# Hybrid attention/convolution encoder layer: the front's sums and low parts all on VectorE, the first block's parts in halves, the second half's rows loaded a step ahead, the convolution behind the third sum

## The chip, the core and the metric

One NeuronCore of a Trainium2 chip runs the whole program in one launch. Its engines are PE (TensorE, matmul), DVE (VectorE), ACT (ScalarE), POOL (GpSimd) and SP (SyncE, which here only issues DMAs). Each runs its own instruction stream in order, and they meet only at semaphores. The metric is the device time of one execution in microseconds, the median of three runs. The profile is a separate execution.

## The reference, cut to what matters

The input is (1, 2048, 1024) in float32. The part of the reference that the change touches is the first norm and the combined projection:

```python
u = rms_norm(x, norm_mix_g[l])
proj = jnp.einsum('bsd,de->bse', u, w_in[l])
q, k, v, bg, cg, hv = jnp.split(proj, ...)          # six parts, each 512 wide
conv = bg * short_conv(cg * hv, conv_w[l])          # centred, width 3, over positions
```

Behind it, outside the change: differential attention over 4 heads with a T5 bias, an RMS norm per head, the output projection with a residual sum, a SwiGLU feed-forward of width 2816 with a residual sum, and a last RMS norm.

## The kernel before, in words

**Precision.** Every float32 matrix product is done as three fp32r products: an operand is split into a high part (ACT copies it to fp32r) and a low part (DVE subtracts the high part from the original), and PE adds hi*hi + hi*lo + lo*hi. So PE needs the low part of an operand, and a low part needs its high part from ACT first.

**The front.** The projection is done for the two halves of the sequence (1024 positions each, of two blocks b = 0, 1 of 512). The 1024 channels are two halves kh = 0, 1 of 4 k-tiles of 128. For the first half, the normed input u is made in place in four tiles `u_raw[b][kh]` of 128 x 2048: `scale_x` (DVE, four instructions of 128 x 512) multiplies by the gain and by 1/rms, which PE has spread over the partitions (`spread_r`). Four output tiles (q) are made plainly: `plain_product(b, tile)`, 24 matmuls each, whose u operands are the splits of the four blocks (`split_block`). `keep_plain` takes each result out of PSUM.

All other output tiles are made in pairs with 7 block products in place of 8: `pair_product(s, k)` for k = 0..6, 12 matmuls each, where s = 0..21 is a step over one pair and one half. Its u operands are three of the blocks and four sums t1..t4 of blocks (`u_slot[k]` holds high and low part of operand k; k = 3, 1, 2, 5 are t1..t4). Before, POOL makes the four sums of the first half (lines 780 to 785), 128 x 2048 each, and `split_sum` splits them (ACT high, DVE low).

**Inside a step** DVE works through a fixed list, `front_step(s)`: the low parts of the seven weight operands of the next step (`split_pair(s + 1, k)`), the sums of the next weights (`sum_pair`), and the sums of the results, `make_u_2`, `make_u_3`, `make_c_22`, `make_c_21`, `make_c_12`, which PE waits for: product k = 5 waits for u_3, k = 6 for c_22, and the next step's k = 2 and 3 for c_21 and c_12. A step whose pair is an input of the convolution is "gated"; `convolve(s)` runs in the step behind it (s = 3, 4, 6, 7 and 17, 18, 20, 21), before directly behind `make_u_2`. In an "out" step (s = 4, 7, 18, 21) `gate_out` multiplies the convolution's result by the third projection, and the next step's first product waits for its first call.

**The second half's input** is made while steps 0 to 8 run. SP loads a row tile (`load_row(n)`, one buffer), ACT squares it (`square`), DVE and POOL make the inverse root (`mean`, `inverse_root`), PE spreads it (`spread_r` in odd steps, behind k = 2). POOL's `make_blocks(i)`, i = 0..3, loads a piece of x (1 MB), issues the DMAs of the scaled blocks to DRAM, makes four sums of 128 x 512 (lines 803 to 809) once DVE has scaled the piece (`scale_piece(i)`, in step 2i + 1), stores the sums, and waits for these stores before it loads the next piece. `load_row(s)` and `load_row(s + 1)` both stand in the even steps of SP's list.

**The turn.** In step 9 SP loads the seven operands of the second half from DRAM (`load_next(k)`, 1 MB each); ACT makes the high parts, DVE the low parts of k = 0, 2, 4, 6 and POOL those of k = 1, 3, 5 (line 820). Step 10 is the first to use them.

The orders are all written out by hand. Behind the front stand attention (PE, DVE, ACT and POOL), the output projection and the feed-forward; the change doesn't touch their code.

## Time and profile before

| | |
|---|---|
| median of 3 runs | 2680.53 us (2679.77 to 2682.09) |
| profiled execution, its own time | 2678.98 us |
| span of that execution | 2677.2 us |
| busy: PE, DVE, ACT, POOL | 97%, 65%, 42%, 22% |
| mean granted TensorE clock | 0.992 |

The span is the time from the first to the last instruction; what lies around it is 1.8 us. The front ends when PE starts on attention, 522 us into the span. A matmul's record shows more than its share of PE's time, because matmuls overlap; the time from one start to the next is what one costs. "Idle before" on a row is how long the engine stood, and what stands behind the arrow is what ended it.

### The profile page before, as it was taken

To read this page: it belongs to the slowest core of one execution; us is meant where nothing else is said; L and a number is where in the kernel's file an instruction comes from. 1 tells how busy PE (TensorE), PEld (TensorE's weight loads), DVE (VectorE), ACT (ScalarE), POOL (GpSimd) and SP (SyncE) were. 2 spreads that over 40 slices of the span, in tenths; PEclk is the share of its full clock that TensorE was granted. 3 is DMA by queue.
4 is the path that set the end of the run, shared out by engine and by line. 5 is a ranking of instruction groups with operands and counts; after the bars stand their busy time and mean duration, and the time that the engine had idled before them with its cause. 6 is when DMAs were issued, how large, how long until landed. Compare 5 with 4: busy or idle time off the path is not lost. (4 is left out here: it accounts for less than half of the span.)

```text
span 2677.2 us, 34138 instructions
## 1 busy us (share of the span) xinstructions
PE 2585.3 (97%) x11920; PEld 2115.3 (79%) x11920; DVE 1739.7 (65%) x2559; ACT 1122.1 (42%) x1588; POOL 586.2 (22%) x394
## 2 busy tenths in 40 slices
PE   7899899989999999999999999999999999999998
PEld 5778788767777777788888888878888888888887
DVE  6788867678888788744476666676566643434354
ACT  4433432266777677632343333343333322323232
POOL 4123200077777777700000000000000000000000
PEclk9999999999999999999999999999999999999999
DMA  6645641412131211156763222342222235656564
GB/s 242 185 170 177 219 149 67 111 45 62 44 82 48 59 44 48 64 169 210 234 189 118 74 90 74 122 150 92 75 90 74 90 134 143 196 158 206 146 209 125
DMA packets 239122, 333.66 MB, mean 125 GB/s; under 512 B 15888, under 2 KB 151568, under 8 KB 234032
## 3 DMA queue, kind: packets, MB, share of 16 engines
q1 hardware_dynamic: 233664, 313.45, 38.4%
q0 software_dynamic: 4544, 17.83, 1.8%
q8 instruction: 56, 0.92, 0.1%
q10 hardware_dynamic: 816, 1.12, 0.1%
q14 instruction: 42, 0.34, 0.0%
HBM read 240.07 MB, written 92.27 MB: 124 GB/s over the span
## 5 line engine op out<-in xcount | busy, mean ns | idle before, releaser
L2136 PE MATMUL banks<-z_hi,w_hi 128*128 128x512 f32 x1116 | 434.5, 389 | 2.3 <-DVE u L1710 1.8
L2136 PE MATMUL banks<-z_hi,w_lo 128*128 128x512 f32 x1116 | 434.2, 389 | 0.0
L2136 PE MATMUL banks<-z_lo,w_hi 128*128 128x512 f32 x1116 | 434.1, 389 | 0.0
L836 POOL TENSOR_TENSOR exp<-exp,exp 128x2048 f32<-128x2048 f32 x64 | 295.8, 4621 | 5.3
L865 POOL TENSOR_TENSOR y_rstd<-y_mean,neg_half 128x1 f32<-128x1 f32 x16 | 9.7, 605 | 1305.8 <-DVE y_mean L1865 1305.8
L1056 ACT ACTIVATE exp<-exp,neg_max 128x2048 f32<-128x2048 f32 x128 | 257.2, 2010 | 34.6 <-DVE neg_max L1583 33.4
L1968 PE MATMUL projected<-u_hi,pair_w_hi 128*128 128x512 f32 x616 | 243.5, 395 | 21.1 <-DVE u_f L1375 7.4
L1160 ACT ACTIVATE w_hi<-w_sum 128x512 fp32r<-128x512 f32 x176 | 111.0, 632 | 328.5 <-PE banks L2136 320.9
L2136 PEld LDWEIGHTS banks<-z_hi,w_hi 128*128 128x128 f32 x1116 | 209.5, 188 | 47.3 <-issue 2.8
L2136 PEld LDWEIGHTS banks<-z_lo,w_hi 128*128 128x128 f32 x1116 | 209.5, 188 | 43.5
L2136 PEld LDWEIGHTS banks<-z_hi,w_lo 128*128 128x128 f32 x1116 | 209.5, 188 | 43.3
L1968 PE MATMUL projected<-u_lo,pair_w_hi 128*128 128x512 f32 x616 | 242.2, 393 | 0.0
L1968 PE MATMUL projected<-u_hi,pair_w_lo 128*128 128x512 f32 x616 | 241.9, 393 | 0.0
L1850 DVE TENSOR_TENSOR hid_lo<-hid_raw,hid_hi 128x512 fp32r<-128x512 f32 x88 | 60.9, 693 | 243.7 <-ACT hid_hi L1258 243.7
L2193 PE MATMUL banks<-down_hi,hid_hi 128*128 128x512 f32 x704 | 216.8, 389 | 0.6 <-DVE down_lo L1853 0.6
L2193 PE MATMUL banks<-down_lo,hid_hi 128*128 128x512 f32 x704 | 216.8, 389 | 0.0
L2193 PE MATMUL banks<-down_hi,hid_lo 128*128 128x512 f32 x704 | 216.7, 389 | 0.0
L1066 ACT ACTIVATE a_t_hi<-tile_turned 128x512 fp32r<-128x512 f32 x256 | 148.1, 600 | 158.8 <-PE tile_turned L2022 158.7
L1595 DVE TENSOR_TENSOR a_t_lo<-tile_turned,a_t_hi 128x512 fp32r<-128x512 f32 x256 | 172.0, 687 | 53.7 <-ACT a_t_hi L1066 53.6
L2004 PE MATMUL scores<-k_sum,q_part_hi 128*128 128x512 f32 x512 | 178.0, 429 | 15.1 <-DVE neg_max L1583 8.4
L1258 ACT ACTIVATE hid_hi<-hid_raw 128x512 fp32r<-128x512 f32 x88 | 55.6, 631 | 320.1 <-PE banks L2193 320.1
L1583 DVE CUSTOM_DVE_ANT_0 exp<-scores,window,half_min 128x1024 f32<-128x1024 f32 x128 | 163.8, 1280 | 31.4 <-PE scores L2004 25.8
(204 smaller groups left out, 5001.3 us busy)
## 6 DMA issues: line engine op xcount, KB each, us to landing
down_raw<-in_w_down SPq DMA_DIRECT2D x88, 512.0 KB, 4.4
pair_raw<-in_w_in SPq DMA_DIRECT2D x24, 1024.0 KB, 6.1
gate_raw<-in_w_gate SPq DMA_DIRECT2D x44, 512.0 KB, 4.5
up_raw<-in_w_up SPq DMA_DIRECT2D x44, 512.0 KB, 5.5
hidden_t<-hid_stage SPq DMA_DIRECT2D x88, 256.0 KB, 2.6
hid_raw<-hidden_t SPq DMA_DIRECT2D x88, 256.0 KB, 3.7
projected_t<-hi_out SPq DMA_DIRECT2D x36, 256.0 KB, 2.8
row_tile<-in_x SPq DMA_DIRECT2D x16, 512.0 KB, 6.1
```

The lines of the kernel that those rows point to most:

```text
L836: nc.gpsimd.tensor_tensor(exp_0[:, slot_0], exp_0[:, slot_0], exp_1[:, slot_1], ALU.add).then_inc(mixed_ready, 1)
L1056: nc.scalar.activation(rows, rows, ACT.Exp, scale=-1.0, bias=neg_max[:, t % 2, part:part + 1], accum_out=exp_sum[:, part, t % 16:t % 16 + ...
L1066: nc.scalar.activation(dst, turned_bank(h, t, index), ACT.Copy).then_inc(group_hi, 1)
L1160: nc.scalar.activation(w_slot[k][0][:, :, :], src, ACT.Copy).then_inc(w_hi_ready_2, 1)
L1258: nc.scalar.activation(hid_part[slot][0][:, :], hid_raw[:, slot], ACT.Copy).then_inc(f_hi_ready, 1)
L1583: nc.vector.tensor_tensor_reduce(out=rows[:, half * HALF:(half + 1) * HALF], in0=scores[:, unit % 2], in1=window[:, window_slice(t, half)] ...
L1595: nc.vector.tensor_tensor(parts[1][at], turned_bank(h, t, index), parts[0][at].bitcast(FP32), ALU.subtract).then_inc(group_lo, 1)
L1850: nc.vector.tensor_tensor(hid_part[slot][1][:, :], hid_raw[:, slot], hid_part[slot][0][:, :].bitcast(FP32), ALU.subtract).then_inc(f_lo_re ...
L1968: last = nc.tensor.matmul(projected[:, PRODUCT_BANK[k]], pair_w[k][w][:, kt], u_slot[k][u][:, kt], start=(kt == 0 and n == 0 and k < 4), s ...
L2004: last = nc.tensor.matmul(scores[:, unit % 2, b * BANK:(b + 1) * BANK], q_part[n][:, (t // 4) % 2, part, t % 4 * P:(t % 4 + 1) * P], k_sum ...
L2136: last = nc.tensor.matmul(c_bank[BANK_OF[k]], w_slot[k][w][:, kt], block[z][:, kt], start=(kt == 0 and t == 0 and k < 4), stop=(kt == 3 an ...
L2193: last = nc.tensor.matmul(y_banks[j][:, c * BANK:(c + 1) * BANK], hid_part[slot][h][:, j * P:(j + 1) * P], down_part[slot][w][:, c * BANK: ...
```

## The change

- `sum_u(n)`: the four sums of the first half move from POOL to DVE, in the order t1, t2, t3, t4 (before: t1, t2, t4, t3), behind the splits of the second block's operands. `u_raw` is placed in other slots, so that each sum can be split while the others are still needed.
- `split_half_block(n)`: `scale_x` of the first block signals after each half (two k-tiles), and its splits go in halves of 128 x 1024 on ACT and DVE. PE waits for them half by half.
- `sum_piece(i)`: the four sums of a piece move from POOL to DVE, to step 2i + 2, where DVE first waits for the stores of the blocks.
- `load_row` of rows 2, 4, 6 moves to the step before (s = 1, 3, 5), ahead of the last stores of that step.
- `split_next(1)`, `(3)`, `(5)` move from POOL to DVE.
- `convolve(s)` moves from behind `make_u_2` to behind `make_c_22`.

```diff
-            b11, b21, b12, b22 = (u_raw[b][kh][:, :, :] for b in range(2) for kh in range(2))
-            nc.gpsimd.tensor_tensor(t1, b12, b11, ALU.subtract).then_inc(u_summed, 1)
...
-                pool.wait_ge(block_stored, 48 * (i + 1))
-                nc.gpsimd.tensor_tensor(p11, p12, p11, ALU.subtract).then_inc(u_summed, 1)
...
+                pool.wait_ge(u_summed, 4 + 4 * i + 4)
...
+            def sum_piece(i):
+                dve.wait_ge(block_stored, 48 * (i + 1))
+                p11, p21, p12, p22 = (piece[:, b, 4 * kh:4 * kh + 4] for b in range(2) for kh in range(2))
+                done = 4 + 4 * i
+                nc.vector.tensor_tensor(p11, p12, p11, ALU.subtract).then_inc(u_summed, 1)
+                dve.wait_ge(u_summed, done + 1)
+                nc.vector.tensor_tensor(p12, p22, p12, ALU.subtract).then_inc(u_summed, 1)
...
@@ SP, front_step(s)
-                if s < 8 and s % 2 == 0:
-                    load_row(s)
+                if s == 0:
+                    load_row(0)
...
                     store_pieces(s, 2, 3)
+                if s < 7 and s % 2:
+                    load_row(s + 1)
@@ DVE, front_step(s)
                 make_u_2(s)
-                convolve(s)
                 if later:
                     split_pair(s + 1, 1)
                 if s == TURN:
-                    split_next(6)
+                    split_next(5)
                 make_u_3(s)
                 if later:
                     split_pair(s + 1, 2)
                 make_c_22(s)
+                if s == TURN:
+                    split_next(6)
+                convolve(s)
+                if s < 9 and s and s % 2 == 0:
+                    sum_piece(s // 2 - 1)
@@ PE, plain_product and pair_product
-                    if tile == 0 and kt % 4 == 0:
-                        pe.wait_ge(u_lo_ready, 2 * b + kt // 4 + 1)
+                    if tile == 0 and kt % 4 == 0 and b:
+                        pe.wait_ge(u_lo_ready, 4 + kt // 4 + 1)
+                    if tile == 0 and kt % 2 == 0 and not b:
+                        pe.wait_ge(u_lo_ready, kt // 2 + 1)
...
-                    if k % 2:
-                        pe.wait_ge(u_lo_pool, k // 2 + 1)
-                    else:
-                        pe.wait_ge(u_lo_ready, 8 + k // 2 + 1)
+                    pe.wait_ge(u_lo_ready, 10 + k + 1)
```

DVE's list at the start of the program before: the two halves of the channels of the first block are scaled (`u_raw_63`, `u_raw_64`), then split into `u_lo_50` and `u_lo_58`.

```order
L1305 SCALAR_TENSOR_TENSOR u_raw_63<-u_raw_63,gain,r_wide 128x512 x4
L1292 SCALAR_TENSOR_TENSOR plain_w_lo_82<-pair_raw_106,plain_w_hi_81 128x1024
L1305 SCALAR_TENSOR_TENSOR u_raw_64<-u_raw_64,gain,r_wide 128x512 x4
L1322 TENSOR_TENSOR u_lo_50<-u_raw_63,u_hi_49 128x2048
L1322 TENSOR_TENSOR u_lo_58<-u_raw_64,u_hi_57 128x2048
```

The same place now:

```order
L1285 SCALAR_TENSOR_TENSOR u_raw_63<-u_raw_63,gain,r_wide 128x512 x4
L1272 SCALAR_TENSOR_TENSOR plain_w_lo_82<-pair_raw_106,plain_w_hi_81 128x1024
L1333 TENSOR_TENSOR u_lo_50<-u_raw_63,u_hi_49 128x1024 x2
L1285 SCALAR_TENSOR_TENSOR u_raw_64<-u_raw_64,gain,r_wide 128x512 x4
L1333 TENSOR_TENSOR u_lo_58<-u_raw_64,u_hi_57 128x1024 x2
```

The first low parts now stand ahead of the second scaling, as two instructions of half the width.

DVE's list in step 4 (and 7), from the sum u_2 (`u_f<-projected,u_f`, first row) on, before:

```order
L1370 TENSOR_TENSOR u_f<-projected,u_f 128x512
L1436 COPY edges<-gated 128x2
L1438 TENSOR_SCALAR conv_y<-gated,taps 128x1023
L1441 SCALAR_TENSOR_TENSOR conv_y<-gated,taps,conv_y 128x1022
L1444 SCALAR_TENSOR_TENSOR conv_y<-gated,taps,conv_y 128x1023
L1364 SCALAR_TENSOR_TENSOR pair_w_lo_92<-pair_sum,pair_w_hi_91 128x512
L1375 TENSOR_TENSOR u_f<-projected,u_f 128x512
L1364 SCALAR_TENSOR_TENSOR pair_w_lo_94<-pair_sum,pair_w_hi_93 128x512
L1381 TENSOR_TENSOR lo_out<-projected,u_f 128x512
```

In step 4 now, from the split behind u_2 on (L1392 is u_3, L1398 is c_22, L1473 the first `gate_out`):

```order
L1381 SCALAR_TENSOR_TENSOR pair_w_lo_92<-pair_sum,pair_w_hi_91 128x512
L1392 TENSOR_TENSOR u_f<-projected,u_f 128x512
L1381 SCALAR_TENSOR_TENSOR pair_w_lo_94<-pair_sum,pair_w_hi_93 128x512
L1398 TENSOR_TENSOR lo_out<-projected,u_f 128x512
L1453 COPY edges<-gated 128x2
L1455 TENSOR_SCALAR conv_y<-gated,taps 128x1023
...
L1311 TENSOR_TENSOR piece<-piece 128x512
L1313 TENSOR_TENSOR piece<-piece 128x512
L1315 TENSOR_TENSOR piece<-piece 128x512
L1317 TENSOR_TENSOR piece<-piece 128x512
L1381 SCALAR_TENSOR_TENSOR pair_w_lo_96<-pair_sum,pair_w_hi_95 128x512
L1381 SCALAR_TENSOR_TENSOR pair_w_lo_98<-pair_raw_107,pair_w_hi_97 128x512
L1473 TENSOR_TENSOR conv_y<-projected,conv_y 128x512
```

The convolution and the four piece sums now stand together between c_22 and the first `gate_out`.

DVE's list at the turn, from the end of step 9 into step 10, before (`u_lo_4_58` is the low part of operand 4, `u_3_f_105` is u_3):

```order
L1396 TENSOR_TENSOR lo_out_115<-projected,u_2_f_104 128x512
L1364 SCALAR_TENSOR_TENSOR pair_w_lo_6_102<-pair_sum_108,pair_w_hi_6_101 128x512
L1352 TENSOR_TENSOR pair_sum_108<-pair_raw_1_107 128x512
L1354 TENSOR_TENSOR pair_sum_108<-pair_sum_108,pair_raw_1_107 128x512
L1334 TENSOR_TENSOR u_lo_4_58<-u_lo_4_58,u_hi_4_57 128x2048
...
L1370 TENSOR_TENSOR u_2_f_104<-projected,u_2_f_104 128x512
L1364 SCALAR_TENSOR_TENSOR pair_w_lo_1_92<-pair_sum_108,pair_w_hi_1_91 128x512
L1334 TENSOR_TENSOR u_lo_6_62<-u_lo_6_62,u_hi_6_61 128x2048
L1375 TENSOR_TENSOR u_3_f_105<-projected,u_2_f_104 128x512
```

The same place now:

```order
L1351 TENSOR_TENSOR u_lo_3_56<-u_lo_3_56,u_hi_3_55 128x2048
L1413 TENSOR_TENSOR lo_out_115<-projected,u_2_f_104 128x512
L1381 SCALAR_TENSOR_TENSOR pair_w_lo_6_102<-pair_sum_108,pair_w_hi_6_101 128x512
L1369 TENSOR_TENSOR pair_sum_108<-pair_raw_1_107 128x512
L1371 TENSOR_TENSOR pair_sum_108<-pair_sum_108,pair_raw_1_107 128x512
L1351 TENSOR_TENSOR u_lo_4_58<-u_lo_4_58,u_hi_4_57 128x2048
...
L1387 TENSOR_TENSOR u_2_f_104<-projected,u_2_f_104 128x512
L1381 SCALAR_TENSOR_TENSOR pair_w_lo_1_92<-pair_sum_108,pair_w_hi_1_91 128x512
L1351 TENSOR_TENSOR u_lo_5_60<-u_lo_5_60,u_hi_5_59 128x2048
L1392 TENSOR_TENSOR u_3_f_105<-projected,u_2_f_104 128x512
```

Operand 3 is now in DVE's list ahead of the end of step 9, operand 5 has taken the place of operand 6 ahead of u_3, and operand 6 stands behind c_22.

## Rows read from the trace of the kernel before

**Rows 1.** Busy time by window (us busy, instructions), granted clock, DMA share, GB/s.
```profile
13.11:312.15 299.04, 268.04 (x1145) 218.21 (x1146) 252.28 (x321) 114.78 (x167) 95.94 (x67) 0.97 0.57 195
78.50:83.00 4.50, 4.49 (x11) 3.52 (x12) 4.50 (x8) 0.00 (x0) 0.00 (x0) 0.50 0.44 162
```

**Rows 2.** Timeline of PE, waits in the front: start, us, engine, line, operation, [idle before].
```profile
22.06 0.76 PE L1937 MATMUL projected<-u_hi,plain_w_hi 128*128 128x512 f32 x1 [8.96 <-DVE u_lo L1322]
52.26 0.50 PE L1937 MATMUL projected<-u_hi,plain_w_hi 128*128 128x512 f32 x1 [0.97 <-DVE u_lo L1322]
78.52 0.79 PE L1968 MATMUL projected<-u_hi,pair_w_hi 128*128 128x512 f32 x1 [6.92 <-DVE pair_w_lo L1364]
139.30 0.47 PE L1968 MATMUL projected<-u_hi,pair_w_hi 128*128 128x512 f32 x1 [3.48 <-DVE lo_out L1381]
176.79 0.47 PE L1968 MATMUL projected<-u_hi,pair_w_hi 128*128 128x512 f32 x1 [1.39 <-DVE u_f L1375]
216.99 0.47 PE L1968 MATMUL projected<-u_hi,pair_w_hi 128*128 128x512 f32 x1 [1.39 <-DVE u_f L1375]
288.99 0.77 PE L1968 MATMUL projected<-u_hi,pair_w_hi 128*128 128x512 f32 x1 [3.24 <-issue]
304.79 0.63 PE L1968 MATMUL projected<-u_hi,pair_w_hi 128*128 128x512 f32 x1 [4.67 <-DVE u_f L1375]
```

**Rows 3.** Timeline of DVE at the start of the program.
```profile
13.22 2.72 DVE L1305 SCALAR_TENSOR_TENSOR u_raw<-u_raw,gain,r_wide 128x512 f32<-128x512 f32 x4 [3.21 <-PE r_wide L1925]
15.86 1.22 DVE L1292 SCALAR_TENSOR_TENSOR plain_w_lo<-pair_raw,plain_w_hi 128x1024 fp32r<-128x1024 f32 x1
19.63 4.49 DVE L1322 TENSOR_TENSOR u_lo<-u_raw,u_hi 128x2048 fp32r<-128x2048 f32 x2
```

**Rows 4.** Timeline of POOL, the first and the last of its four sums of blocks.
```profile
43.47 6.59 POOL L780 TENSOR_TENSOR u_sum<-u_raw,u_raw 128x2048 f32<-128x2048 f32 x1 [15.89 <-DVE u_raw L1305]
61.65 5.05 POOL L785 TENSOR_TENSOR u_sum<-u_raw,u_raw 128x2048 f32<-128x2048 f32 x1
```

**Rows 5.** Timeline of DVE beside these sums.
```profile
46.46 5.74 DVE L1322 TENSOR_TENSOR u_lo<-u_raw,u_hi 128x2048 fp32r<-128x2048 f32 x1
52.13 0.68 DVE L1340 TENSOR_TENSOR lo_out<-projected,hi_out 128x512 fp32r<-128x512 f32 x1
52.73 4.49 DVE L1352 TENSOR_TENSOR pair_sum<-pair_raw 128x512 f32<-128x512 f32 x1
62.16 5.09 DVE L1356 TENSOR_TENSOR pair_sum<-pair_raw 128x512 f32<-128x512 f32 x1
67.78 2.28 DVE L1329 TENSOR_TENSOR u_lo<-u_sum,u_hi 128x2048 fp32r<-128x2048 f32 x1
```

**Rows 6.** Timeline of ACT, the wait for a row in step 2.
```profile
136.16 1.06 ACT L884 ACTIVATE row_tile<-row_tile 128x1024 f32<-128x1024 f32 x1 [7.04 <-DMA row_tile<-in_x]
```

**Rows 7.** Timeline of DVE, first and behind last instruction of a convolution.
```profile
171.73 0.22 DVE L1436 COPY edges<-gated 128x2 f32<-128x2 f32 x1
175.36 0.69 DVE L1364 SCALAR_TENSOR_TENSOR pair_w_lo<-pair_sum,pair_w_hi 128x512 fp32r<-128x512 f32 x1
```

**Rows 8.** Timeline of POOL, last sum of piece 1, next piece's load, its root.
```profile
167.84 1.62 POOL L809 TENSOR_TENSOR piece<-piece 128x512 f32<-128x512 f32 x1
178.20 0.56 POOL L793 DMA_DIRECT2D piece<-in_x_second  x1 [5.14 <-DMA u_blocks<-piece]
182.03 0.94 POOL L771 TENSOR_TENSOR rstd<-mean_eps,neg_half 128x1 f32<-128x1 f32 x1 [3.27 <-DVE mean_eps L1297]
```

**Rows 9.** Timeline of SP's queue and of ACT at the turn.
```profile
264.03 8.48 SPq L457 DMA_DIRECT2D u_lo<-u_blocks  x4
271.87 1.92 ACT L901 ACTIVATE u_hi<-u_lo 128x2048 fp32r<-128x2048 f32 x1 [1.77 <-DMA u_lo<-u_blocks]
```

**Rows 10.** Timeline of DVE at the turn, the instructions beside POOL's.
```profile
277.33 4.96 DVE L1364 SCALAR_TENSOR_TENSOR pair_w_lo<-pair_raw,pair_w_hi 128x512 fp32r<-128x512 f32 x1
282.81 6.08 DVE L1334 TENSOR_TENSOR u_lo<-u_lo,u_hi 128x2048 fp32r<-128x2048 f32 x1
294.33 5.10 DVE L1364 SCALAR_TENSOR_TENSOR pair_w_lo<-pair_raw,pair_w_hi 128x512 fp32r<-128x512 f32 x1
```

More of the change, by code:

```diff
@@ L1012, in _ @@
             split_plain(0)
-            split_block(0)
-            split_block(1)
+            for n in range(4):
+                split_half_block(n)
             split_plain(1)
@@ L1298, in mean, with scale_x @@
                                         ALU.mult, ALU.add).then_inc(mean_ready, 1)
[L1300 removed]
+            def scale_x(b, kh, kts=range(4)):
                 dve.wait_ge(r_ready, 4 * b + 4)
                 dve.wait_ge(x_loaded[b][kh], 16)
[L1303 removed]
+                for kt in kts:
                     rows = u_raw[b][kh][:, kt]
```

131 lines of the change are left out of this document (73 added, 58 removed).

## Prediction, made before the changed kernel was run

> **What bounds the kernel now.** I began with the windows table, then the timeline of PE alone, reading only the rows that carry an idle time, and then the timelines of DVE, POOL, ACT and SP around each of them. The reader should see that PE is the bound nearly everywhere, so a change can only win where PE stands or runs slowly, and that the front is where it does. From the last instruction that spreads the first root to the end of step 10, PE is busy 268.0 of 299.0 us at a mean granted clock of 0.97 [rows 1]. PE's waits there are eight [rows 2]: 8.96, 0.97, 6.92, 3.48, 1.39, 1.39, 3.24 and 4.67, together 31.0 us. Behind three of them the matmuls also start long (0.79, 0.77, 0.63 us where others start with 0.47): the clock has fallen to its lower level, 1.2 GHz, and the window behind the wait of 6.92 shows it, 0.50, with 11 matmuls in 4.5 us [rows 1]. From 176.79 to 216.99 PE does 14 products of 12 matmuls, one wait of 1.39 and some 0.6 of spreading, so one product is 38.2 / 14 = 2.73 us, a matmul 0.227 and a step of seven products 19.1. At the lower level a matmul costs 0.41.
>
> Why DVE is late in front of the 6.92: POOL's four sums run from 43.47 to 66.7 [rows 4], and DVE's instructions with both inputs in SBUF crawl beside them: a low part of 128 x 2048 takes 5.74 where the same one later takes 2.28, and three of the weight sums (two shown) take 4.5 to 5.1 where 128 x 512 needs 0.6 from start to start [rows 5]. The instruction at 52.13, which has one input in PSUM, takes 0.68 beside the same sum of POOL [rows 5]. The Trainium skill's page "SBUF — State Buffer" (section "Who interferes with whom") has the rule for it: DVE and GpSimd share one pair of ports, as an exclusive lock, which a DVE instruction with two SBUF inputs needs and one with a single one doesn't. By that rule the two engines never worked side by side there at all, so a sum moved to DVE costs its own time and no more; if they had shared bandwidth, moving it would win less. The trace agrees, as far as these rows go.
>
> I set T for the start of a step on PE, and take 0.6 for a DVE instruction of 128 x 512 [rows 5] and 2.24 for one of 128 x 2048 (two in 4.49) [rows 3].
>
> **The change, part by part.**
>
> First block in halves. Before, DVE scales (2.72), does a weight part (1.22), scales again, and has the first low part at about 21.9; PE starts at 22.06 [rows 2, 3]. Now ACT can start on the first half after two of the four scalings (14.6) and is done by 15.7; DVE is through with scaling and weight part at 17.1 [rows 3] and makes a low part of 128 x 1024. No row has that instruction; half of 2.24 is 1.12, the weight part of the same width 1.22 [rows 3]; I take 1.15. PE starts at 18.3, 3.8 us earlier. What is late next: the third quarter, behind one low part, four scalings and one more low part (19.4 + 2.7 + 1.1 = 23.2), while PE, slow at first as now, is through with two quarters at 22.4. It waits 0.8. Gain 3.0.
>
> The sums on DVE. Contention goes: 3.5 us of the low part and 12.9 of the three weight sums, 16.4; four sums of 2.24 come, 9.0. DVE is also 3 us earlier. Counted through: second scaling done at 40.3, two low parts 44.7, `keep_plain` 45.3, four sums to 54.2. The wait of 0.97 goes, since the last low part of the second block is there at 44.7 and PE wants it at 48. `plain_product(1, 3)`, the one that now waits behind the sums (through `keep_plain(0, 3)`, at 54.8), begins at 62. Then to the first three weight parts at 64.3, and PE ends the plain products at 67.3; so step 0 starts at 67.3 against 78.52 and nothing is late: 11.2, of which 3.0 is above and 8.2 here. With the wait of 6.92 gone the clock doesn't fall: 11 matmuls at 0.41 in place of 0.227, 2.2. DVE is through with step 0's parts at about 73, six microseconds after PE has begun, where it was five before; that brings the row for ACT's square, loaded behind them, close to PE's k = 6. I put 0.2 for it, bounds 0 and 2.
>
> Rows a step ahead. In step 2 ACT waits 7.04 for a row [rows 6], which holds up the high part of the third weight operand, c_22 behind it, and PE by 3.48 [rows 2]. Loaded ahead of step 1's last stores the row is some 15 us earlier: 3.5 gained. Nothing stands behind this load in SP's queue but stores with three steps' slack; if the store were late by the 0.4 us of an issue, nobody would ask.
>
> Convolution behind c_22. It is 3.6 us of DVE (171.73 to 175.36) [rows 7], and PE's two waits of 1.39 are for u_3, right behind it [rows 2]. They go: 2.8. In its place the first `gate_out` is late. In step 4, c_22 can't be made before product 3 ends, T + 10.9, so c_22 at T + 11.6, convolution to 15.2, piece sums (four, chained by their semaphores, 0.73 each) to 18.1, two weight parts 19.3, `gate_out` 19.9; the next step wants it at 19.1. Cost 0.8. In step 7, which has 3.2 us of scaling in place of the sums, 1.1 by the same count, because its c_22 is late (below). Steps 18 and 21 have neither sums nor scaling: `gate_out` is there at 17.0.
>
> Piece sums. Before, POOL's last one ends at 169.46, and it issues the next piece's load at 178.20, 8.7 later, with the root behind it [rows 8]. That was early in the step; now the sums end at T + 18.1 in steps 4 and 6. Load issue, two roots (0.56 + 0.94 + 0.55) put the second root at T + 28.9, and PE wants it behind product k = 2 of the next step, T + 19.1 + 8.2 = T + 27.3. The wait: 0.8 in step 5 (it starts 0.8 late anyway) and 1.8 in step 7 (sums a little later). In step 2 there is no convolution, the sums end at 15, and nobody waits. DVE now waits itself for the block stores; behind it stand the weight parts of the next step. The stores have 14 us from the scaling to the sums, and POOL's wait for stores of that kind was 5.1 behind 3.3 of issuing [rows 8], so nothing. The contention in the four pieces (about 4 us of DVE each) goes and pays for the 2.9.
>
> The turn. Before: two waits, 3.24 and 4.67 [rows 2], and 12 and 8 matmuls at the lower clock, 20 x 0.2 = 4.0 plus 0.5 in the change between: 12.4 us. DVE loses 16.1 - 3.4 = 12.7 us beside POOL [rows 10] and now gets three low parts, 6.7. But the seven loads start a little later: the last sums end at T9 - 4.5 (T9: start of step 9), their stores are there at about T9 + 4, where the first load went out at T9 + 2.7 before; 1.3 late. It landed 7.8 after its issue [rows 9]. So ACT's first high part ends at T9 + 13.8 and DVE goes on at 14.4: five low parts, six instructions of 128 x 512 and the next weights' first sums (1.4) bring it to 30.7 for operand 4, and PE wants that at 29.9: wait 0.8. Five short ones with operand 5's low part among them: u_3 at 36.5, PE wants it at 33.5: wait 3.0. Operand 6's low part is there at 39.9: wait 0.7. Together 4.5 in place of 12.4: 7.9. Bounds: 12.4 (no wait is left) and 4 (the clock falls again, and DVE runs 1.5 late).
>
> **The sum.** 3.0 + 8.2 + 2.2 + 3.5 + 2.8 = 19.7; less 0.2 + 0.8 + 1.1 + 0.8 + 1.8 = 4.7; plus 7.9: 22.9. Behind step 10 the steps had no wait of PE, and attention and feed-forward keep their code. The profiled execution took 2678.98, so 2656 in its terms; the median of the runs shown is 1.5 above it: 2657.5.
>
> **A page against the turn's number.** After a wait of 3.24 the clock fell and after one of 3.48 it didn't [rows 2], so the wait of 3.0 that I expect ahead of product 5 may or may not cost it. Taken as a fall, it is 8 to 12 matmuls at 0.41, 1.6 to 2.4 us, and the time 2659.5. The Trainium skill's "TensorE: Matmul & The Clock Gate" (Part 1, "The HAM clock gate") says that an idle PE is throttled to half rate until it has been busy for a while, by a count that runs freely and doesn't start with the wait. By that rule the fall is possible; the trace, with one case of either kind, agrees.
>
> **The rivals.**
>
> A: the pieces' chain is longer. POOL's wait for the stores was 8.7 us in the one shown; with the stores behind row and weight loads it can be 10 or more, and then the piece itself is late for its scaling too, and with it the blocks for step 9. Against it: SP's queue is quieter where the sums now end. Price: 1.4 more in each of steps 3, 5 and 7, 2 in c_21, and 1.4 at the turn: gain 15 to 17, 2664.
>
> B: the turn wins little. The loads share the DMA engines and land later than DVE could use them. For it: ACT waited for the first of them [rows 9]. Against: it didn't for the next three, and DVE was the late one. Then the turn gives 3 in place of 7.9: 2662.
>
> C: nothing takes the place of the waits, because DVE, some 17 us of work lighter than in the contended trace, catches up everywhere: 19.7 + 12.4 less a little: 2650.
>
> D: slower. DVE stands in `sum_piece` for the block stores, in order, with c_21, c_12 and all weight parts behind it. Each microsecond over the 14 that the stores have costs PE nearly one, four times. At 20 us from scaling to landing the whole gain is gone, and from there it is slower; at 24, 2680.5 - 23 + 40 = 2697. Nothing speaks for 20 where such stores took 8.4.
>
> E: the change doesn't do what it says. POOL keeps only roots of 128 x 1 and DMA issues, so it can't contend with sums; that part can't fail. That the half parts win nothing could be, if the second weight half of the block isn't in yet: the 3.0 would go, 2660.5, inside the range.
>
> **Numbers.** Forecast as above, 2653 to 2661: 0.55. A: 0.18. B (or E): 0.13. C: 0.08. D: 0.03, and 0.03 for a loss that I don't see which eats the gain up to no change. Likeliest time 2657.5. Range from C's 2650 to 2667, A and B together with the clock. A measurement of this kernel can tell about 0.2%, 5.4 us, from no change: faster by more 0.94, within it 0.03, slower by more 0.03.
>
> **What would show it.** PE's first matmul of the plain products at about 18.3 with a short wait a few microseconds later; step 0 near 67 without idle time ahead of it and no window at 0.50 there; no idle time in step 2, none for u_3 in steps 4 and 7, but short ones ahead of steps 5 and 8, and ahead of PE's spreading in steps 5 and 7; at the turn a wait of about 3 for u_3; step 10 done near 289 in place of 312. DVE's weight sums all near 0.69. Wrong it would be by a long wait of DVE ahead of a piece's first sum, by POOL's load of a piece more than 10 us behind the sums, or by PE standing at step 9 for operand 0.

## The result, and the profile after

The changed kernel takes 2652.39 us (median of 4 runs, 2651.64 to 2652.76), the kernel before 2681.31 (4 runs, 2679.77 to 2683.09): ratio 0.9894, 95% interval 0.9881 to 0.9906. The forecast was 2657.5 with a range from 2650 to 2667; the time lies in the range, 5.1 under the likeliest value and 0.6 under the band of the main case (2653 to 2661). Profiled execution against profiled execution it is 2678.98 to 2652.76, 26.2 us, where the terms gave 22.9.

The page of the changed kernel, span and busy time:

```profile
span 2650.7 us, 34146 instructions
PE 2578.1 (97%) x11920; PEld 2110.8 (80%) x11920; DVE 1720.6 (65%) x2584; ACT 1122.7 (42%) x1590; POOL 521.8 (20%) x371
```

POOL lost 64 us, and DVE, which took over all of that work, is 19 us less busy: its own instructions no longer stretch. The timeline of PE in the front from the first plain matmul on, every row that carries an idle time, and the first row of attention:

```profile
19.00 0.77 PE L1970 MATMUL projected<-u_hi,plain_w_hi 128*128 128x512 f32 x1 [5.25 <-DVE u_lo L1333]
...
85.46 0.47 PE L1998 MATMUL projected<-u_hi,pair_w_hi 128*128 128x512 f32 x1 [1.18 <-DVE lo_out L1398]
...
166.66 0.47 PE L1998 MATMUL projected<-u_hi,pair_w_hi 128*128 128x512 f32 x1 [0.82 <-DVE conv_y L1473]
...
226.19 0.47 PE L1998 MATMUL projected<-u_hi,pair_w_hi 128*128 128x512 f32 x1 [1.17 <-DVE conv_y L1473]
...
280.87 0.47 PE L1998 MATMUL projected<-u_hi,pair_w_hi 128*128 128x512 f32 x1 [2.75 <-DVE u_f L1392]
...
498.58 0.70 PE L2034 MATMUL scores<-k_sum,q_part_hi 128*128 128x512 f32 x2 [0.94 <-DVEq L1601]
```

The eight waits of [rows 2], 31.0 us, have become five, 11.2 us. Attention starts at 498.58 where it started at 522.50: 23.9 us of the span are won in the front. Windows of the changed kernel (the front from the first plain matmul to the last of step 21; the six microseconds behind the wait of 2.75; 4 us early in attention; 15 us at its end):

```profile
19.00:496.80 477.80, 471.80 (x2066) 387.75 (x2067) 368.12 (x554) 175.04 (x270) 31.36 (x44) 1.00 0.50 166
...
280.80:286.80 6.00, 5.93 (x19) 4.75 (x20) 6.00 (x8) 1.64 (x3) 0.00 (x0) 0.72 0.22 85
514.00:518.00 4.00, 3.55 (x13) 3.06 (x14) 0.69 (x1) 0.60 (x1) 3.92 (x5) 0.57 0.00 0
1106.80:1121.80 15.00, 11.43 (x50) 9.71 (x50) 4.88 (x9) 5.11 (x10) 7.16 (x3) 0.66 0.52 206
```

And the kernel before, its front, 8 us early in its attention and the 15 us at its end:

```profile
22.06:520.70 498.64, 476.59 (x2065) 390.91 (x2066) 383.32 (x525) 172.50 (x268) 95.94 (x67) 0.98 0.47 156
536.00:544.00 8.00, 5.67 (x18) 4.72 (x19) 2.73 (x7) 3.93 (x5) 7.92 (x5) 0.57 0.00 0
1130.70:1145.70 15.00, 11.12 (x42) 9.24 (x43) 5.07 (x9) 4.90 (x9) 7.58 (x3) 0.54 0.56 223
```

The span is 26.5 shorter, so 2.6 us came from behind the front, from code that is the same. The rows show where it can come from: early in attention and where it ends, PE stands now and then and the clock falls, in both kernels, but for a shorter time in the changed one (0.57 over 8 us against 0.57 over 4; 0.54 with 42 matmuls in 15 us against 0.66 with 50). In the profiles below the stretch at the end has 0.54 to 0.77, whatever the edit, and what lies between the end of the front and the end of the span is anything from 2152.5 to 2156.5 us; and the runs of one kernel lie up to 5.5 us apart, those of the kernel before up to 8.6. I therefore compare kernels by the time in the span at which the last of step 21's matmuls of the kind `u_hi,pair_w_hi` starts, called the end of the front here, as well as by the median. The 95% interval of a ratio below is some 4 us to either side, so two versions of the changed kernel whose medians are 4 us apart or less can't be told apart by their times; what is said of such a pair rests on the profiled execution of each, its waits and the end of its front. It stands in the source view of that line, which for the changed kernel reads (x and min/median/max ns, first and last start):

```profile
L1998 PE MATMUL projected<-u_hi,pair_w_hi x616: 387/389/628, 67.8 to 496.8; 128*128 128x512 f32 x154
```

### The profile page after: what moved, and what is told of

Same layout as the page of the kernel before. It is cut to its first block and busy times, and to the rows that moved or that the text cites. A ratio compares the mean times of both kernels' runs of the same rounds, so it can differ in the third digit from the quotient of the medians.

```text
span 2650.7 us, 34146 instructions
## 1 busy us (share of the span) xinstructions
PE 2578.1 (97%) x11920; PEld 2110.8 (80%) x11920; DVE 1720.6 (65%) x2584; ACT 1122.7 (42%) x1590; POOL 521.8 (20%) x371
```

## The experiments

"Changed" is the changed kernel, 2652.4 us, end of the front 496.8; the kernel before has 520.7. Each row is a kernel of its own, timed beside the kernel before (its median there 2680.7 to 2681.1). The last column counts the places in the front, behind the first plain products, where windows of 4 us have a granted clock under 0.97; the changed kernel has one, the kernel before three.

| kernel | median us | ratio, 95% | end of front | waits of PE behind its start | falls |
|---|---|---|---|---|---|
| no halves | 2655.2 | 0.9908 (0.9893 to 0.9923) | 498.8 | 1.18, 0.82, 1.16, 1.77, 0.35 | 0 |
| sums on POOL | 2659.1 | 0.9923 (0.9909 to 0.9936) | 500.9 | 3.60, 0.44, 0.81, 1.16, 2.23, 0.35 | 1 |
| turn on POOL | 2659.7 | 0.9927 (0.9913 to 0.9940) | 502.8 | 1.70, 0.81, 1.17, 2.63, 3.59 | 2 |
| pieces on POOL | 2652.5 | 0.9898 (0.9883 to 0.9913) | 495.8 | 1.85, 0.24, 1.17, 2.27, 0.35 | 0 |
| rows in even steps | 2656.1 | 0.9910 (0.9897 to 0.9924) | 500.0 | 0.44, 1.66, 2.68, 1.16, 2.32 | 2 |
| convolution in front | 2650.3 | 0.9887 (0.9872 to 0.9902) | 495.0 | 1.84, 2.47, 0.35 | 1 |
| pieces and convolution | 2654.7 | 0.9902 (0.9887 to 0.9917) | 496.0 | 0.49, 1.58, 1.39, 1.39, 2.05, 0.37 | 0 |
| rows and convolution | 2650.6 | 0.9887 (0.9872 to 0.9902) | 493.4 | 0.64, 2.56, 0.37 | 0 |
| before, convolution late | 2678.3 | 0.9995 (0.9986 to 1.0004) | 525.6 | 0.97, 6.92, 3.80, 0.23, 1.17, 2.81, 5.75 | 4 |
| before, rows ahead | 2674.9 | 0.9977 (0.9966 to 0.9987) | 518.1 | 0.98, 6.91, 1.40, 1.39, 2.79, 5.82 | 3 |
| two repairs | 2647.9 | 0.9878 (0.9863 to 0.9893) | 492.2 | 2.72 | 1 |
| three repairs | 2645.3 | 0.9867 (0.9852 to 0.9882) | 488.7 | 0.26 | 0 |

**Whole blocks again.**

```diff
-            scale_x(0, 0, (0, 1)); scale_x(0, 0, (2, 3)); split_plain(0); split_half_block(0); split_half_block(1)
-            scale_x(0, 1, (0, 1)); scale_x(0, 1, (2, 3)); split_half_block(2); split_half_block(3)
+            scale_x(0, 0); split_plain(0); scale_x(0, 1); split_first_block(0); split_first_block(1)
```

> The changed kernel (2652.4) with the first block scaled and split in whole tiles again: four scalings, the weight part, four scalings, then two low parts of 128 x 2048. Everything else stays. Theory (the path through the first low part sets PE's start, and PE is the bound from there on, so the start moves everything): PE's first plain matmul at about 22.7 in place of 19.0, and nothing behind it catches up, so the time is 3.7 longer: about 2656. Rival (my case E: the start is hidden, something later, such as the second half of the block or step 0's operands, sets the end): PE starts 3.7 later, but the time is within 1 of 2652.4, with a wait gone further on.

The start of PE in this kernel:

```profile
22.73 0.77 PE L1964 MATMUL projected<-u_hi,plain_w_hi 128*128 128x512 f32 x1 [8.95 <-DVE u_lo L1331]
```

3.7 later. The end of the front is 2.0 later, the median 2.8: the wait for u_3 at the turn is 1.77 in place of 2.75, and behind it the clock didn't fall, 1.3 more (worked out below, at the turn). Up to there the products are 4.0 later (170.65 against 166.66 at the start of step 5). So the start is on the path and the rival falls, but the theory's "nothing behind it catches up" fails too: the turn takes back 1.0 of wait and the fall.

**The four sums of the first half on POOL.**

```diff
@@ POOL, behind the roots (DVE's four calls of sum_u go)
+            for n in range(4):
+                sum_u(n)      # nc.gpsimd.tensor_tensor in place of nc.vector
```

> The changed kernel with the four 128 x 2048 sums of the first half back on POOL, in the new order t1, t2, t3, t4; places and order of the splits stay as in the changed kernel. Theory (DVE's instructions with two inputs in SBUF stand while POOL works on such a sum): low parts and weight sums of DVE at 4 to 6 us beside the sums, a wait of PE of 5 to 8 ahead of step 0, a fall of the clock behind it worth 2.2; 8 to 10 longer, 2661 to 2663. Rival (order: the gain came from the earlier splits of blocks 2 and 3 and the new places, which this kernel keeps): step 0 starts within 2 of where it does in the changed kernel, 2653 to 2655.

POOL's first and last sum, and DVE beside and behind the sums:

```profile
40.87 8.79 POOL L785 TENSOR_TENSOR u_sum<-u_raw,u_raw 128x2048 f32<-128x2048 f32 x1 [11.48 <-DVE u_raw L1305]
...
59.66 4.63 POOL L793 TENSOR_TENSOR u_sum<-u_raw,u_sum 128x2048 f32<-128x2048 f32 x1
```

```profile
42.90 2.29 DVE L1342 TENSOR_TENSOR u_lo<-u_raw,u_hi 128x2048 fp32r<-128x2048 f32 x1
...
50.24 4.98 DVE L1374 TENSOR_TENSOR pair_sum<-pair_sum,pair_raw 128x512 f32<-128x512 f32 x1
64.39 2.29 DVE L1349 TENSOR_TENSOR u_lo<-u_sum,u_hi 128x2048 fp32r<-128x2048 f32 x1 [9.16 <-POOL u_sum L793]
```

Step 0 starts at 71.33 behind a wait of 3.60, 3.5 later than in the changed kernel; the end of the front is 4.1 later, the median 6.7. (The fall of the clock in step 0 costs 2.8 here: from its start to the wait ahead of product 6 the step takes 19.3, in the changed kernel 16.5. Smaller waits in step 0 and at the turn, and no fall there, give most of it back.) So of the 11.4 us that step 0 starts earlier in the changed kernel, 3.7 are the halves, 3.8 the engine (3.5, and the 0.25 by which PE began earlier here), and the other 3.9, by subtraction, the new order and places; no kernel with the old order and the sums on DVE was run. Both theories hold a part. Two of DVE's weight sums crawl as expected, but its low part at 42.90 takes 2.29 as ever, and there it is POOL's sum that stretches, to 8.79 where the last takes 4.63. And in this order DVE has little to do there and stands 9.16 for POOL's last sum: what costs here is the length of POOL's chain, 23 us against DVE's 9.

**The low parts 1, 3 and 5 at the turn on POOL.**

```diff
-                if s == TURN:
-                    split_next(5)
...
-                if s == TURN - 1:
-                    split_next(1)
...
-                if s == TURN - 1:
-                    split_next(3)
@@ POOL
+            for k in (1, 3, 5):
+                split_next(k)
```

> The changed kernel with the low parts of operands 1, 3 and 5 at the turn back on POOL, operand 6 still behind c_22. Theory (contention with POOL was what made DVE late, not its amount of work): DVE's instructions beside POOL's at 5 to 6 us, two waits of PE in step 10 (or one in step 9 and one in step 10) of 7 to 8 together where the changed kernel has 2.75, and a slow clock behind one or both, 4 more: 9 to 10 longer, about 2662. Rival (my case B: the landing of the loads sets the turn): 3 longer or less, 2655.

DVE in this kernel, a weight part and a low part of the turn, and PE's two waits:

```profile
261.57 5.01 DVE L1389 SCALAR_TENSOR_TENSOR pair_w_lo<-pair_raw,pair_w_hi 128x512 fp32r<-128x512 f32 x1
...
267.10 6.09 DVE L1359 TENSOR_TENSOR u_lo<-u_lo,u_hi 128x2048 fp32r<-128x2048 f32 x1
```

```profile
273.29 0.77 PE L2003 MATMUL projected<-u_hi,pair_w_hi 128*128 128x512 f32 x1 [2.63 <-issue]
...
286.90 0.74 PE L2003 MATMUL projected<-u_hi,pair_w_hi 128*128 128x512 f32 x1 [3.59 <-DVE u_f L1400]
```

The stretch and both waits with a slow clock are back, 6.0 at the end of the front and 7.3 in the median against 9 to 10 expected; the turn's term stands, rival B (the landing) falls. The size may be smaller because operand 6 stays behind c_22 here, so that DVE has one low part fewer in front of u_3 than before; no run shows that by itself.

**The piece sums on POOL.**

```diff
-                if s < 9 and s and s % 2 == 0:
-                    sum_piece(s // 2 - 1)
@@ POOL, make_blocks(i), behind the stores of the blocks
+                sum_piece(i)
```

> The changed kernel with the four 128 x 512 sums of each piece back on POOL, behind its wait for the block stores. Theory (my count: the sums cost DVE 2.9 a piece and contention cost it about 4, both with slack but for the first gate_out): the wait of 0.82 ahead of step 5 goes, that of 1.17 ahead of step 8 stays, and no other wait comes, as the convolution now stands behind u_3: 2651 to 2653, no difference that can be told. Rival (contention reaches a sum that PE waits for): waits of 1 to 3 in steps 2, 4, 6 or 8 behind instructions of DVE of 2 us or more, 2655 to 2660. POOL's wait for its stores of the sums, 2.4 to 2.7 in the changed kernel, back to 5 or more, as the sums end early in the step again beside the other loads; if it stays under 3, the time in the step does not matter.

POOL's next loads behind the stores of the sums of pieces 0, 1 and 2:

```profile
127.84 0.57 POOL L797 DMA_DIRECT2D piece<-in_x_second  x1 [6.52 <-DMA u_blocks<-piece]
...
165.69 0.57 POOL L797 DMA_DIRECT2D piece<-in_x_second  x1 [2.44 <-DMA u_blocks<-piece]
...
202.22 0.57 POOL L797 DMA_DIRECT2D piece<-in_x_second  x1 [4.65 <-DMA u_blocks<-piece]
```

No difference, as the theory said, though the wait ahead of step 5 is 0.24 and not gone. DVE is busy 4.6 us more from 20 to 300 us than in the changed kernel though 11.6 us of sums left it, 4 a piece as I had counted, all of it under cover. At the turn the clock stays up here, which is where the earlier end of the front comes from. POOL's wait for stores is anything from 2.4 to 6.5 in this one kernel, and it goes with the place in the step: the sums end 9.2, 12.6 and 7.8 behind the start of their step for 6.52, 2.44 and 4.65. In the changed kernel they end 14.5 to 18.1 behind it, with waits of 2.43 to 2.67, and in the kernel before 7.8 to 9.2, with 5.14 to 6.89.

**Rows in the even steps.**

```diff
-                if s == 0:
-                    load_row(0)
+                if s < 8 and s % 2 == 0:
+                    load_row(s)
...
-                if s < 7 and s % 2:
-                    load_row(s + 1)
```

> The changed kernel with the rows 2, 4 and 6 loaded in the even steps again, in front of nothing but that step's stores. Theory (the load stands too late in SP's list, so ACT waits for it and c_22 with it): the wait of 3.48 for c_22 in step 2 is back, nothing in steps 4 and 6, as before; the end of the front 3.5 later, about 2656. Rival (the quieter front has brought the row in time anyway): a wait under 1 in step 2, 2652 to 2653.

ACT's waits for the rows of steps 2 and 4, DVE behind the second, and PE ahead of step 5:

```profile
120.64 1.06 ACT L856 ACTIVATE row_tile<-row_tile 128x1024 f32<-128x1024 f32 x1 [5.54 <-DMA row_tile<-in_x]
...
157.57 1.06 ACT L856 ACTIVATE row_tile<-row_tile 128x1024 f32<-128x1024 f32 x1 [4.20 <-DMA row_tile<-in_x]
```

```profile
159.28 0.69 DVE L1379 SCALAR_TENSOR_TENSOR pair_w_lo<-pair_sum,pair_w_hi 128x512 fp32r<-128x512 f32 x1 [3.05 <-ACT pair_w_hi L907]
```

```profile
168.81 0.77 PE L1996 MATMUL projected<-u_hi,pair_w_hi 128*128 128x512 f32 x1 [2.68 <-DVE conv_y L1471]
```

3.7 in the median and 3.2 at the end of the front, the size that the theory said, and for another reason: in step 2 no idle time of PE is shown. It stands ahead of step 5, since DVE has stood 3.05 for the weight part behind the row and has the convolution and four sums still to do before `gate_out`, and the clock falls behind that wait. A right size was no proof of the mechanism here.

**The convolution back behind u_2.**

```diff
                 make_u_2(s)
+                convolve(s)
...
                     split_next(6)
-                convolve(s)
```

> The changed kernel with the convolution back behind u_2. Theory (it only moves 3.6 us of DVE from in front of u_3 to in front of the first gate_out): the two waits of 1.39 for u_3 are back in steps 4 and 7, and those of 0.82 and 1.17 ahead of steps 5 and 8 are gone, so 2.8 less 2.0: 0.8 longer, which can be seen in the starts of the steps and not in the time. Rival (the weight parts and c_22 behind u_3 come late as well): 3 or more longer, with waits in two products of a step.

DVE in step 4 of this kernel, the last part of the convolution, the weight part and u_3:

```profile
157.39 1.29 DVE L1461 SCALAR_TENSOR_TENSOR conv_y<-gated,taps,conv_y 128x1023 f32<-128x1023 f32 x1
158.59 0.69 DVE L1381 SCALAR_TENSOR_TENSOR pair_w_lo<-pair_sum,pair_w_hi 128x512 fp32r<-128x512 f32 x1
159.19 0.69 DVE L1392 TENSOR_TENSOR u_f<-projected,u_f 128x512 f32<-128x512 f32 x1
```

Both theories fail. The two waits of 1.39 do not come back, those of 0.82 and 1.17 are gone, and the front ends 1.8 earlier than in the changed kernel although the clock falls in step 0 (the median is 2.1 lower; the intervals of the two ratios overlap). So my term of 2.8 for the convolution wasn't earned by the convolution alone. The next kernel asks what earned it.

**Pieces on POOL and the convolution in front, together.** The two diffs above in one kernel.

> The changed kernel with two parts undone together: the piece sums on POOL and the convolution behind u_2. Each alone cost nothing (2652.5 and 2650.3 against 2652.4) and neither brought the waits of 1.39 back. Theory (the waits of 1.39 came from both together: POOL's piece sums lengthened four of DVE's instructions by 4.2, and the convolution stood in front of u_3, so that either edit removes them): with both undone the two waits for u_3 are back, 2.8 longer than the kernel with the convolution alone undone: 2653. Rival (something else in the change removed them, such as the rows or the earlier start): no wait for u_3 in steps 4 and 7, 2650.

DVE in step 4 beside POOL's piece sums, and PE's two waits:

```profile
148.23 1.79 DVE L1437 TENSOR_TENSOR gated<-lo_out 128x512 f32<-128x512 f32 x1
149.94 1.78 DVE L1370 TENSOR_TENSOR pair_sum<-pair_raw 128x512 f32<-128x512 f32 x1
151.76 1.67 DVE L1372 TENSOR_TENSOR pair_sum<-pair_sum,pair_raw 128x512 f32<-128x512 f32 x1
153.35 1.78 DVE L1382 SCALAR_TENSOR_TENSOR pair_w_lo<-pair_raw,pair_w_hi 128x512 fp32r<-128x512 f32 x1
```

```profile
161.91 0.47 PE L1997 MATMUL projected<-u_hi,pair_w_hi 128*128 128x512 f32 x1 [1.39 <-DVE u_f L1393]
...
202.14 0.47 PE L1997 MATMUL projected<-u_hi,pair_w_hi 128*128 128x512 f32 x1 [1.39 <-DVE u_f L1393]
```

The waits are back to the hundredth. (The end of the front is 1.0 later than with the convolution alone undone, and not 2.8: there the clock fell once, in step 0, which cost 1.3, and here never, and the waits in step 0 and at the turn are 0.3 and 0.4 shorter here.) They needed both: four instructions that took 7.0 where they take 2.8, and the convolution in front of u_3. The changed kernel removes both causes, and pays for the second with the late `gate_out`.

The profile of the kernel before had shown it already. Its waits of 1.39 lie in steps 4 and 6, not in 4 and 7 as the prediction and the expectations have them: the second is at 216.99 [rows 2], and steps 6 and 7 start here:

```profile
201.84 0.39 PE L1968 MATMUL projected<-u_hi,pair_w_hi 128*128 128x512 f32 x1
...
222.55 0.39 PE L1968 MATMUL projected<-u_hi,pair_w_hi 128*128 128x512 f32 x1
```

The convolution stands in front of u_3 in steps 3, 4, 6 and 7, and POOL makes a piece's sums in steps 2, 4, 6 and 8 (from 122.13, 162.93, 202.97 and 243.36). PE waits for u_3 only in the two steps that have both.

**Rows in the even steps and the convolution in front, together.**

> The changed kernel with the rows in the even steps and the convolution behind u_2. With the rows alone undone, ACT waited 5.54 and 4.20 for rows in steps 2 and 4, but PE stood only ahead of step 5 (2.68, for the gate_out behind convolution and sums), 3.7 longer in all. Theory (DVE stands for the weight part that follows the row, and the convolution put there in front of it fills that time): no wait above 0.5 in steps 2 to 5, 2650 to 2651, so the rows a step ahead are worth nothing without the convolution's new place. Rival (the row holds up c_22 itself): a wait of 2 to 3.5 in step 2 or 4, 2653 to 2654.

No wait from step 1 to step 9, although ACT still waits 5.54 for the row in step 2. The front ends at 493.4, 1.6 earlier than with the convolution alone in front, where the clock fell in step 0. The rows a step ahead are worth nothing once the pieces have left POOL and the convolution is in front.

**One part alone in the kernel before.** First the convolution:

```diff
                 make_u_2(s)
-                convolve(s)
...
                 make_c_22(s)
+                convolve(s)
```

> The kernel before with only the convolution moved behind c_22. Theory (DVE has too much to do in steps 4 and 7 beside POOL, and its first gate_out ended at 179.6, when step 5 began): the waits of 1.39 for u_3 go, waits of 1 to 1.4 for the first gate_out ahead of steps 5 and 8 come, so 0 to 0.8 shorter. Rival (my term as predicted, both waits gone and only small ones in their place): 2.0 to 2.8 shorter, about 2678.

The ratio is 0.9995, no difference that can be told. The two waits of 1.39 are gone and 0.23 and 1.17 stand ahead of steps 5 and 8: 1.4 less wait, where the theory had 0 to 0.8 and my term's count of the same edit 0.9 (2.8 less 1.9). In the profiled execution the clock fell a fourth time, behind the wait in step 2, which was 3.80 here, which cost 2.7 (step 2 less its wait: 21.7 against 19.0); step 0 began 1.7 later, its fall was longer, the waits at the turn were 0.6 longer, and the front ended 4.9 later than in the profile of the kernel before. So the 1.4 is seen in the waits and not in the time.

Then the rows (the lines of the diff above, the other way):

> The kernel before with only the rows 2, 4 and 6 loaded a step ahead. Theory (my term): ACT does not wait for the row in step 2, PE's wait of 3.48 for c_22 goes, and nothing comes for it: 3.5 shorter, about 2677. Rival (DVE beside POOL's piece sums in step 2 is late anyway): a wait of 1.5 or more stays in step 2 or 3, 2 or less shorter, 2679.

The wait of 3.48 goes and nothing comes for it in steps 2 and 3; the end of the front is 2.6 earlier, 3.0 reckoned from PE's start; the ratio says 6 us. The two profiled executions differ by 3.2 in the span, so only 0.6 of that lies behind the front, and the other 3 us are in executions that no profile shows. In the kernel before the rows were worth about their term in the front. There the row was issued at 128.29, 9.0 behind the start of step 2 (119.34); in the kernel with rows in even steps at 114.28, 5.9 behind it (108.37). In SP's list a store of one of DVE's results (`lo_out`, third row below) stands ahead of it, and DVE had lost 3.1 us beside POOL's sums of piece 0 (rows of the kernel before):

```profile
122.22 1.75 DVE L1352 TENSOR_TENSOR pair_sum<-pair_raw 128x512 f32<-128x512 f32 x1
124.00 1.67 DVE L1354 TENSOR_TENSOR pair_sum<-pair_sum,pair_raw 128x512 f32<-128x512 f32 x1
125.59 1.78 DVE L1404 TENSOR_TENSOR lo_out<-u_f,hi_out 128x512 fp32r<-128x512 f32 x1
```

So POOL's sums stand behind this wait too, as far as these rows go; no kernel with only the piece sums moved was run.

**Two repairs.**

```diff
                 convolve(s)
+                gate_out(s, 0)
...
                 keep_lo(s, 0, 2)
-                gate_out(s, 0)
@@ SP
+                if s == 0:
+                    load_row(0)
                 if s + 2 < N_STEPS:
                     load_pair(s + 4)
-                if s == 0:
-                    load_row(0)
```

> Two repairs of the changed kernel: the first gate_out directly behind the convolution, ahead of the piece sums and scalings and two weight parts; and the first row of the second half issued ahead of the load of pair 4 in SP's list. Theory (both waits are only order): the waits of 0.82 and 1.17 ahead of steps 5 and 8 and of 1.18 in step 0 go, and nothing comes for them but at most 0.5 in step 5 behind POOL's root, as the piece sums end 0.6 later; 3.2 shorter, 2649.5. Rival (the row is late by its 6 to 8 us in flight beside a piece of 1 MB, not by its place in the list): the wait in step 0 stays over 0.8, and the gain is 2 or less, 2650.5 to 2651.

All three waits go. ACT's square comes at 79.65 in place of 82.32, and that suffices. 4.6 earlier at the end of the front, 4.5 in the median; the first step alone starts as before (67.8). That is 1.4 more than the 3.2 of the waits. The starts of the steps place it: a step with a wait in it, or right behind one, also takes a little longer beside the wait (step 0 less its wait takes 19.49 in the changed kernel and 19.04 here, and 0.1 to 0.2 each in steps 1, 4, 5, 7 and 8), 1.1 together, and the fall at the turn is 6 matmuls long and not 8, 0.3.

**Three repairs.**

```diff
@@ DVE, s == TURN, behind split_next(4), in place of the old order of the same calls
+                make_u_2(s); split_next(5); make_u_3(s); make_c_22(s); split_next(6)
+                split_pair(s + 1, 0); keep_lo(s, 3, 1); keep_lo(s, 0, 2)
+                sum_pair(s + 1, 1); split_pair(s + 1, 1); split_pair(s + 1, 2)
@@ ACT, s == TURN
+                keep_hi(s, 3, C22); keep_first(s); split_pair(s + 1, 2); split_pair(s + 1, 3)
```

> The kernel of the two repairs with a third: in step 10 (the turn's) DVE makes operand 5's low part, u_3, c_22 and operand 6's low part ahead of the next step's weight parts and sums, and ACT keeps the results ahead of the next step's third and fourth weight part. Theory (DVE is the late one there and 2.4 us of its work ahead of u_3 can wait): PE's wait of 2.75 falls to under 0.5, the clock does not fall behind it (1.0 more), and steps 11 and 12 have waits of under 0.5: 3 to 3.5 shorter than the kernel of the two repairs, about 2646. Rival (the work is only pushed on, and step 11's first products wait for it): as much wait in step 11 as was won, 2649.5.

PE's wait at the turn in the kernel of two repairs, and below it the one wait that is left in this one:

```profile
276.58 0.77 PE L1998 MATMUL projected<-u_hi,pair_w_hi 128*128 128x512 f32 x1 [2.72 <-DVE u_f L1392]
```

```profile
293.39 0.47 PE L2009 MATMUL projected<-u_hi,pair_w_hi 128*128 128x512 f32 x1 [0.26 <-DVE u_f L1395]
```

3.5 earlier at the end of the front, 2.6 in the median. This kernel, 2645.3 us, beats the kernel before and the changed one (its slowest run, 2646.1, against the fastest of the changed kernel, 2651.6), and its front has no wait of PE above 0.3 behind the first matmul.

## Why the prediction was right, and where it was not

By its own steps, each in the profiled executions:

- **Halves**, 3.0: PE starts 3.06 earlier although this execution's DVE started 0.64 later (13.86 against 13.22), so 3.7. The wait of 0.8 for the third quarter did not come: DVE made its low part at 22.54, before the slow matmuls of two quarters were through. That was close: in two of the later kernels with the same code there it came, with 0.44 and 0.49.
- **Sums on DVE**, 8.2, and the clock, 2.2: step 0 starts at 67.8 against 78.52, with the halves 11.4 where 11.2 was forecast, no idle time and no slow clock. The size is right. About half of it is the new order, by subtraction, and not the engine.
- **Row in step 0**, 0.2: it was 1.18, inside the bounds of 0 and 2. The prediction worked out no time in flight for the row; it took 7.8, issued behind pair 4. Rows of SP and ACT in the changed kernel:

```profile
74.51 0.37 SPq L434 DMA_DIRECT2D row_tile<-in_x  x1
```

```profile
82.32 1.06 ACT L858 ACTIVATE row_tile<-row_tile 128x1024 f32<-128x1024 f32 x1 [6.56 <-DMA row_tile<-in_x]
```

- **Rows ahead**, 3.5, and **convolution**, 2.8: the waits went, and `gate_out` came late by 0.82 and 1.17 (0.8 and 1.1 forecast). But I gave each wait to the one edit that stands next to it. The experiments show that the waits for u_3 had two causes together, POOL's piece sums and the convolution's place, and for the row's wait the rows say the same of POOL's sums, without a run. The step of the prediction that is wrong is this: the contention in the four pieces had its share in these waits, and I had priced its leaving at nothing ("pays for the 2.9"). The sum came out because the change removed all the causes; as a forecast of either edit alone it fails in the changed kernel's setting, where the convolution's new place costs 2 of waits, and the rows a step ahead are worth 3.2 only beside that place and nothing without it. That these 6.3 us came out was in part luck: the sum holds because all the causes went together, and not because each edit earned its own term.
- **Spreading in steps 5 and 7**, 0.8 and 1.8: neither came. I took 8.7 us from the last sum to the next load from [rows 8] (of which 5.14 is the wait for the stores; rival A calls the whole 8.7 that wait); it was 5.7, with a wait for the stores of 2.44:

```profile
165.00 2.93 POOL L794 DMA_DIRECT2D u_blocks<-piece  x4 [15.88 <-DVE piece L1317]
170.37 0.57 POOL L784 DMA_DIRECT2D piece<-in_x_second  x1 [2.44 <-DMA u_blocks<-piece]
```

  This is the term that was sized wrong, by 2.6, and most of the distance in the front. The 5.14 was read where the sums end early in a step (7.8 behind its start), the new chain has them at 18.1 behind it, and there the wait is half as long; the prediction said that the old chain was early in the step, and kept its price. Rival A, which made the same chain longer, had the wrong sign.
- **Turn**, 7.9: one wait of 2.75 (3.0 forecast for u_3), none for operands 4 and 6 (0.8 and 0.7), because the first load went out at T9 + 2.9 (248.23 less 245.32) as before (264.03 less 261.11; the prediction has 2.7), and not 1.3 later. The clock fell behind it: from product 5 to the end of the front it is 216.0 here and 215.0 with pieces on POOL, where the clock stayed up and 0.35 of waiting is in it; so the fall cost 1.3. 12.4 less 2.75 less 1.3: 8.4.

Together 3.7 + 7.7 + 2.2 + 3.5 + 2.8 + 8.4 = 28.3, less 1.2 and 2.0: 25.1, against 23.9 + 0.6 for the late start = 24.5 measured in the front; 22.9 was forecast. (The 0.6 between them is what steps 0 and 1 take beside the wait of 1.18.) So the front was forecast 1.0 to 1.6 short, and that is the difference of errors that go both ways: 2.6 of spreading that didn't come and 1.0 of row that did. The other 2.6 of the span lie behind the front, and 1.9 more of the distance of 5.1 is only that the profiled execution was 1.5 under its kernel's median before and is 0.4 above it now. That attention would take the same time was the one sentence about it, and the clock early in it and at its end decided otherwise. Whether a given start of attention brings the shorter or the longer slow stretch is left open: no run was made for it.

Rivals B and D found nothing for them: DVE never stood in `sum_piece` for the stores of the blocks. Rival C's 2650, a front without waits, is reached and passed by the repairs. The changed kernel's time is nearer to C's than to the likeliest one, but not for C's reason: waits of 5.9 us took the place of the old ones, and what brought it there is mostly the 2.6 and the 1.9 above, which no term foresaw.

The rule of the Trainium skill ("SBUF — State Buffer", section "Who interferes with whom") is borne out by the kernels with large POOL tensor operations in them: 1.18 to 1.79 for DVE's 128 x 512 with two SBUF inputs beside POOL's 128 x 512 of 1.62, 4.98 and 6.09 beside POOL's 128 x 2048, 0.68 for those with one input in PSUM. Either engine can be the one that stands: POOL's sum of 8.79 beside two low parts of DVE at 2.29 each. There the four sums ran from 40.87 to 64.29, 23.4 us, which is four of 4.63 alone plus 4.9, where DVE's instructions with two SBUF inputs in that time take some 4.4 and 1.2 by themselves.

## What to carry to other kernels

A wait can have two causes, and then each of two edits removes it alone: before both are made, ask what each costs once the other is in, and undo them one at a time when both are. When an engine stops slowing another down, look again at every reordering that was meant to cover the slowness; here one had become a loss of 2 us, and one was worth something only beside it. Before guessing at the second cause, lay the steps that wait beside the like steps that don't. An instruction that the next step waits for (`gate_out`, a row for ACT) belongs ahead of work with slack in an in-order list, and two such moves took 4.6 us off the end of the front here.

## What the runs showed of the hardware

- The clock and the length of a wait. Behind waits of 1.84, 2.32, 2.63, 2.68, 2.72, 2.75, 2.79 and 2.81 PE's clock went to its lower level for 6 to 8 matmuls, behind waits of 1.85, 2.23, 2.27, 2.47 and 2.56 it did not, nor behind 3.48 in [rows 2]. The closest pair is the same product of step 0 in two kernels, 4 us each; first behind the wait of 1.84 (convolution in front), then of 1.85 (pieces on POOL):

```profile
86.00:90.00 4.00, 3.94 (x12) 3.20 (x13) 3.15 (x6) 2.04 (x4) 0.34 (x1) 0.69 0.73 151
```

```profile
86.00:90.00 4.00, 3.79 (x16) 2.87 (x17) 3.30 (x7) 1.95 (x4) 0.19 (x1) 1.00 0.67 150
```

  The length alone doesn't decide it. That agrees with a count that doesn't start with the wait (the Trainium skill, "TensorE: Matmul & The Clock Gate", Part 1, "The HAM clock gate"). The falls, 1.0 to 1.8 us each where they are that short and 2.3 to 2.8 in the longer ones, decide as much of a comparison of two good kernels as the waits do.
- POOL's wait for four stores of 256 KB behind its issues: 3.5 to 7.0 in the 13 cases, in five kernels, in which the sums end 7.8 to 9.3 us behind the start of a step, and 2.4 to 2.8 in 26 of the 29 in which they end 12.6 or more behind it (3.4 to 3.7 in the other three). Why it is so isn't shown; a value of such a wait is a price only for its own place in the step.
- The first row of the second half, 512 KB, from issue to use: 7.4 to 8.5 in the eight kernels that have the first half's sums on DVE and issue it right behind a 1 MB weight load (7.8 in the changed one), 6.3 to 7.1 in the four with these sums on POOL and the same order, and 6.3 (79.65 less 73.34) in both that issue it right ahead of the load.
